# Identity turns by TensorE in the pauses at stage borders, semaphores of several stages cleared together, and the first mix squares ahead of attention's last store

## The reference, cut to what matters

```python
h = rmsnorm(x, g_mix[l])
proj = h @ w_in[l] + b_in[l]                       # queries, keys, values of both groups
...                                                # rotary on group A
oa = window_sink_gqa(qa, ka, va, sinks[l])
ob = chunk_relbias_attention(qb, kb, vb, rel_bias[l])
mix = jnp.concatenate([rmsnorm(oa, g_grp_a[l]), rmsnorm(ob, g_grp_b[l])], axis=-1)
x = x + mix @ w_out[l]
h = rmsnorm(x, g_cross[l])
x = x + memory_cross_attention(h, rmsnorm(mem, g_mem[l]), w_cq[l], w_ckv[l], w_co[l])
h = rmsnorm(x, g_ffn[l])
x = x + (jax.nn.silu(h @ w_gate[l]) * (h @ w_up[l])) @ w_down[l]
return rmsnorm(x, g_final)
```

## Time and profile before

| what | value |
|---|---|
| median of three runs | 2836.86 us (2836.58 to 2837.24) |
| the profiled execution's own time | 2837.78 us |
| its span, first to last instruction | 2836.0 us |
| PE busy | 2760.0 us, 97% of the span |
| DVE, ACT, POOL busy | 1587.8, 1064.3, 1065.7 us |
| mean granted TensorE clock | 0.990 |

### The profile page before, as it was taken

One profiled execution on the slowest core, in us unless ns is written; L12 is line 12 of the kernel. 1 busy time (PEld: TensorE's weight loads), 2 busy tenths in 40 slices (PEclk: granted clock), 3 DMA queues, 4 the chain that ended last, 5 costly groups with the idle time before them and its releaser, 6 DMA issues.

```text
span 2836.0 us, 39240 instructions
## 1 busy us (share of the span) xinstructions
PE 2760.0 (97%) x14112; PEld 2338.4 (82%) x14112; DVE 1587.8 (56%) x2721; ACT 1064.3 (38%) x2101; POOL 1065.7 (38%) x754
## 2 busy tenths in 40 slices
PE   8999999999999999999998999999999999999998
PEld 8888888899999787788887788888888887888876
DVE  3356664566688332333335766668866666654364
ACT  5433333366666221332334333334333332222342
POOL 7644454210000111321214645555654553552251
PEclk9999999999999999999999999999999999999999
DMA  7657768755664434122226333335432335644453
GB/s 269 239 166 261 258 210 260 209 145 149 165 141 112 176 133 155 75 67 80 79 82 210 109 93 104 112 112 186 126 98 92 106 112 191 234 140 145 142 177 126
DMA packets 244599, 428.47 MB, mean 151 GB/s; under 512 B 17856, under 2 KB 151488, under 8 KB 239168
## 3 DMA queue, kind: packets, MB, share of 16 engines
q1 hardware_dynamic: 207008, 358.43, 39.8%
q10 hardware_dynamic: 37408, 67.65, 7.6%
HBM read 285.50 MB, written 135.27 MB: 148 GB/s over the span
## 4 chain that ended last, share of the span: by engine, by line
PE 54%; DVE 2%; DMA 1%; POOL 1%; ACT 1%; issue 1%; SPq 0%; POOLq 0%; ACTq 0%; DVEq 0%
PE gu_acc L51 9%; PE gu_acc L52 9%; PE gu_acc L53 9%; PE down_acc L51 4%; PE down_acc L52 4%; PE down_acc L53 4%; PE cross_sum_s L51 2%; PE cross_sum_s L53 2%; PE cross_sum_s L52 2%; PE cross_sum_o L51 2%; PE cross_sum_o L53 2%; PE cross_sum_o L52 2%; DVE shared_m L2828 1%; DVE gu_t L2469 0%; PE cross_turned L2147 0%
## 5 line engine op out<-in xcount | busy, mean ns | idle before, releaser
L51 PE MATMUL gu_acc<-gu_t,shared_m 128*128 128x512 f32 x704 | 275.5, 391 | 4.8 <-DVE gu_t L2469 4.8
L53 PE MATMUL gu_acc<-gu_t,shared_m 128*128 128x512 f32 x704 | 274.9, 390 | 0.0
L52 PE MATMUL gu_acc<-gu_t,shared_m 128*128 128x512 f32 x704 | 274.9, 390 | 0.0
L338 POOL TENSOR_TENSOR front_wq_lo<-front_wq_raw,front_wq_hi 128x1024 fp32r<-128x1024 f32 x72 | 179.9, 2500 | 206.8 <-ACT front_wq_hi L334 206.6
L2412 ACT ACTIVATE shared_m<-kept_x 128x512 fp32r<-128x512 f32 x175 | 109.3, 628 | 211.6 <-PE gu_acc L53 191.0
L51 PEld LDWEIGHTS gu_acc<-gu_t,shared_m 128*128 128x128 f32 x704 | 132.8, 189 | 34.7 <-issue 4.4
L53 PEld LDWEIGHTS gu_acc<-gu_t,shared_m 128*128 128x128 f32 x704 | 132.7, 189 | 27.7
L52 PEld LDWEIGHTS gu_acc<-gu_t,shared_m 128*128 128x128 f32 x704 | 132.8, 189 | 27.3
L334 ACT ACTIVATE front_wq_hi<-front_wq_raw 128x1024 fp32r<-128x1024 f32 x72 | 76.2, 1058 | 191.9 <-PE qkv_acc L53 104.6
L51 PE MATMUL gu_acc<-shared_m 128*128 128x512 f32 x352 | 137.8, 391 | 2.9 <-POOL shared_m L2385 2.5
L52 PE MATMUL gu_acc<-shared_m 128*128 128x512 f32 x352 | 137.7, 391 | 0.0
(11 more groups left out here) (342 smaller groups left out, 7838.6 us busy)
## 6 DMA issues: line engine op xcount, KB each, us to landing
front_wq_raw<-in_w_in ACTq DMA_DIRECT2D x69, 512.0 KB, 4.2
ahead_w_even<-in_w_gate SPq DMA_DIRECT2D x44, 512.0 KB, 4.5
kept_x<-in_w_up SPq DMA_DIRECT2D x44, 512.0 KB, 4.3
a_d<-gu_a_mix SPq DMA_DIRECT2D x88, 256.0 KB, 3.2
a_d<-gu_a SPq DMA_DIRECT2D x66, 256.0 KB, 4.3
kept_x<-in_w_down SPq DMA_DIRECT2D x56, 256.0 KB, 4.7
shared_m<-a_d SPq DMA_DIRECT2D x19, 704.0 KB, 4.3
beside_turned<-a_d SPq DMA_DIRECT2D x19, 704.0 KB, 4.1
```

The costliest lines, as they stand in the source:

```text
L51: pe.matmul(out, l_hi, r_hi, start=first, stop=False)
L52: pe.matmul(out, l_hi, r_lo, start=False, stop=False)
L53: return pe.matmul(out, l_lo, r_hi, start=False, stop=last)
L338: pool.tensor_tensor(self.lo[:, i % Q_SLOTS, :], self.raw[:, i % Q_SLOTS, :], raw(self.hi[:, i % Q_SLOTS, :]), ALU.subtract).then_inc(self ...
```

## The change

`idle_turns` is new: it transposes the identity by itself into a PSUM bank that holds nothing needed. It is called in eight places, 182 turns in ten groups. A new class `Ends` gathers the semaphores of several rooms and clears them with one close; three of them stand where fourteen closes stood: after qkv, after mix, and at the program's end. Nothing is closed after products and after attention. And in attention's ACT stream `store_last(1)` moves behind the first squares of mix.

```diff
+class Ends:
+    def __init__(self, nc):
+        self.nc, self.sems = nc, []
+
+    def close(self):
+        self.nc.clear_and_free_semaphores(self.sems)
+        self.nc.all_engine_barrier()
...
     def sem(self, name):
         semaphore = self.nc.alloc_semaphore(f"{self.stage}_{name}")
-        self.sems.append(semaphore)
+        self.ends.sems.append(semaphore)
         return semaphore
-
-    def close(self):
-
-        self.nc.clear_and_free_semaphores(self.sems)
-        self.nc.all_engine_barrier()
...
+def idle_turns(pe, bank, ident, n):
+    for _ in range(n):
+        pe.transpose(bank[:, 0:P], ident[:, :], ident[:, :])
...
                 pe.wait_ge(s_ident, 2)
+                idle_turns(pe, acc[ACCS - 1], ident, 40)
                 for n in range(MT):
                     rows.turn(pe, ident[:, :], n)
+                    idle_turns(pe, acc[ACCS - 1], ident, 12 if n == 0 else 8)
                 pe.wait_ge(rows.s_lo, 2 * MT)
...
                         if a == TURN[t]:
                             rows.turn(pe, ident[:, :], MT + t)
+                pe.wait_ge(rows.s_lo, 2 * (MT + BT))
+                idle_turns(pe, rows.turned[0], ident, 18)
...
                         last.then_inc(s_vt, 1)
+                acc_free(TOTAL - ACCS)
+                idle_turns(pe, acc[TOTAL % ACCS], ident, 16)
...
-                store_last(1)
                 act.wait_ge(s_wlo, KT)
                 norm.start_act(act)
                 norm.act_square(act, 0, 0, 0)
+                store_last(1)
...
                     if step == NB:
                         norm.start_pe(pe)
+                after(pe, s_max, NB - 1)
+                idle_turns(pe, sum_s[NB % 2], ident, 30)
...
                 norm.pe_turn(pe, ident[:, :], 0, 0)
+                idle_turns(pe, acc[0], ident, 10)
...
                 over_pairs(pe, PAIRS, pair)
+                idle_turns(pe, norm.turned[0], ident, 10)
...
             def scores(n):
+                if n < 2:
+                    idle_turns(pe, sum_o[0], ident, 28 if n else 10)
                 pe.wait_ge(s_xlo, 2 * n + 2)
...
+    first_ends, middle_ends, last_ends = Ends(nc), Ends(nc), Ends(nc)
     with ExitStack() as later:
+        later.callback(last_ends.close)
...
+            first_ends.close()
...
+        middle_ends.close()
```

More of the change, by code:

```diff
@@ L58, in raw, with __init__ @@
     return ap.bitcast(F32)
+class Ends:
[4 more added lines that the diff above has]
+        self.nc.all_engine_barrier()
 class Room:
-    def __init__(self, nc, ctx, stage, side="left", ends=None):
-        self.nc, self.ctx, self.stage, self.sems, self.side = nc, ctx, stage, [], side
-        (ends or ctx).callback(self.close)
+    def __init__(self, nc, ctx, stage, ends, side="left"):
+        self.nc, self.ctx, self.stage, self.ends, self.side = nc, ctx, stage, ends, side
         self.s_gate = self.sem("s_gate")
@@ L342, in stage_products @@
 def stage_products(nc, mem, g_mem, g_cross_t, w_k, w_v, w_cq_t, w_co, m_d, n_d, x, g_mix, ident, gain_x, s_gain_x,
-                   h0, weights):
+                   h0, weights, ends):
     with ExitStack() as ctx:
-        room = Room(nc, ctx, "prod")
+        room = Room(nc, ctx, "prod", ends)
         rows = Rows(room)
@@ L1084, in __init__, with stage_attention @@
         self.norm = Norm(kept, 2, self.rows, self.s_rows, self.raw)
-def stage_attention(nc, qk_d, v_d, mix_d, bias_d, sinks8, weight, first, s_qk_stored, s_v_stored):
+def stage_attention(nc, qk_d, v_d, mix_d, bias_d, sinks8, weight, first, s_qk_stored, s_v_stored, ends):
     JOBS = [("b", h) for h in range(8)] + [("a", pp) for pp in range(N_PAIR)]
@@ L1158, in stage_attention @@
     with ExitStack() as ctx:
-        room = Room(nc, ctx, "att")
+        room = Room(nc, ctx, "att", ends)
         ident, norm = weight.ident, weight.norm
@@ L1509, in rows_of, with stage_mix @@
     return tensor[n * P:(n + 1) * P, :] if isinstance(n, int) else tensor[bass.ds(n * P, P), :]
-def stage_mix(nc, mix_d, x, weight, x2_d, m_sb, s_mlo, m_d, x2, s_x2, s_st, ident_next, s_ident_next):
+def stage_mix(nc, mix_d, x, weight, x2_d, m_sb, s_mlo, m_d, x2, s_x2, s_st, ident_next, s_ident_next, ends):
     with ExitStack() as ctx:
-        room = Room(nc, ctx, "mix")
+        room = Room(nc, ctx, "mix", ends)
         norm, ident = weight.norm, weight.ident
@@ L1757, in stage_cross @@
     with ExitStack() as ctx:
-        room = Room(nc, ctx, "cross", ends=ends)
+        room = Room(nc, ctx, "cross", ends)
         n_sb = [room.sb(f"n{part}", [P, KT, D], F32R) for part in range(2)]
@@ L2591, in stage_down @@
     with ExitStack() as ctx:
-        room = Room(nc, ctx, "down", ends=ends)
+        room = Room(nc, ctx, "down", ends)
         AHEAD = first.AHEAD
@@ L2931, in build @@
                 stage_products(nc, a["mem"], a["g_mem"], a["g_cross_t"], a["w_xk"], a["w_xv"], a["w_cq_t"], a["w_co"],
-                               m_d, n_d, a["x"], a["g_mix"], ident, gain, s_gain, h0, weights)
+                               m_d, n_d, a["x"], a["g_mix"], ident, gain, s_gain, h0, weights, first_ends)
                 stage_qkv(nc, a["x"], ident, gain, first, h0, weights, a["b_in"], a["positions"], a["freq"],
-                          a["rel_rev"], ext_d, bias_d, qk_d, v_d, s_qk_stored, s_v_stored)
-            weight = OutWeights(Room(nc, ctx, "wout", "right"), a["w_out"], a["g_grp"])
-            stage_attention(nc, qk_d, v_d, mix_d, bias_d, a["sinks"], weight, first, s_qk_stored, s_v_stored)
+                          a["rel_rev"], ext_d, bias_d, qk_d, v_d, s_qk_stored, s_v_stored, first_ends)
+            first_ends.close()
+            weight = OutWeights(Room(nc, ctx, "wout", middle_ends, "right"), a["w_out"], a["g_grp"])
+            stage_attention(nc, qk_d, v_d, mix_d, bias_d, a["sinks"], weight, first, s_qk_stored, s_v_stored,
+                            middle_ends)
             until_mix.close()
-            shared = Room(nc, later, "shared")
+            shared = Room(nc, later, "shared", last_ends)
             m_sb = [shared.sb(f"m{part}", [P, KT, D], F32R) for part in range(2)]
             s_mlo = shared.sem("s_m_lo")
-            kept = Room(nc, later, "kept")
+            kept = Room(nc, later, "kept", last_ends)
             x2 = kept.sb("x2", [P, XB, D])
@@ L2946, in build @@
             s_ident = kept.sem("s_ident")
-            stage_mix(nc, mix_d, a["x"], weight, x2_d, m_sb, s_mlo, m_d, x2, s_x2, s_x2_stored, ident, s_ident)
-        beside = Room(nc, later, "beside")
+            stage_mix(nc, mix_d, a["x"], weight, x2_d, m_sb, s_mlo, m_d, x2, s_x2, s_x2_stored, ident, s_ident,
+                      middle_ends)
+        middle_ends.close()
+        beside = Room(nc, later, "beside", last_ends)
         turned = [beside.sb(f"turned{part}", [P, 2, KT * P], F32R) for part in range(2)]
-        operands = GateUpOperands(shared, m_sb, Room(nc, later, "ahead", "right"), x2, turned, a["w_gate"], a["w_up"],
+        operands = GateUpOperands(shared, m_sb, Room(nc, later, "ahead", last_ends, "right"), x2, turned, a["w_gate"], a["w_up"],
                                   t_d)
         with nc.Block() as block:
-            cross = stage_cross(nc, block, later, ident, s_ident, turned, s_x2_stored, x2_d, x2, s_x2, m_sb, s_mlo, n_d,
+            cross = stage_cross(nc, block, last_ends, ident, s_ident, turned, s_x2_stored, x2_d, x2, s_x2, m_sb, s_mlo, n_d,
                                 a["g_ffn"], x3_d, t_d, operands)
             rows = DownOperands(shared, operands, a_d, a["w_down"])
-            gate_up = stage_gate_up(nc, block, later, cross, t_d, a["w_gate"], a["w_up"], a_d, operands, rows)
-            stage_down(nc, block, later, gate_up, a_d, x3_d, a["w_down"], a["g_final"], out, rows)
+            gate_up = stage_gate_up(nc, block, last_ends, cross, t_d, a["w_gate"], a["w_up"], a_d, operands, rows)
+            stage_down(nc, block, last_ends, gate_up, a_d, x3_d, a["w_down"], a["g_final"], out, rows)
 def by_tile(w, width):
```

10 lines of the change are left out of this document (5 added, 5 removed).

## The result

| | before | after |
|---|---|---|
| median of five runs each, us | 2836.86 | 2819.82 |
| lowest to highest, us | 2833.68 to 2838.34 | 2817.46 to 2824.29 |
| profiled execution, us | 2837.78 | 2817.46 |
| its span, us | 2836.0 | 2815.7 |
| PE busy in the span, us | 2760.0 | 2767.0 |

The ratio is 0.9943, with a 95% interval of 0.9932 to 0.9953: faster by 0.57%. The time forecast, 2818.2, is 1.6 us from the median. The profiled execution of after is the fastest of its five, so its gain of 20.3 us is above the median's 17.0. PE's busy time rose although the kernel is faster: 182 turns of the identity now count as busy.

What follows compares the result with a forecast made beforehand. PE was taken to bound the kernel: its work, its pauses and its half-clock stretches. Terms 3.35 + 2.65 + 1.75 + 4.0 + 3.2 + 3.75 = 18.7 us took the median from 2836.86 to 2818.2, range 2813.5 to 2824.5.

Steps and rivals of the forecast that it cites:

- The start: First products: full clock gives 2.7 us, faster real turns 0.7 (bounds 0 and 1.76); 3.35 in all, bounds 1.5 and 4.5.
- rival 3: All idle turns: turning an identity does not count as work for the clock; 2839.0 us, slower than before; chance 0.03.
- Products to qkv: Border products to qkv: the close going gives 0.6 us, the clock holding over a 2.1 us pause 2.05; sum 2.65.
- Rival 1: The clock falls in pauses left behind products, behind qkv and in mix: 2.05, 1.3, about 1.5 lost; 2823.0 us; chance 0.17.
- qkv to attention: Border qkv to attention: second close gone, 0.45 us; clock 1.3, between 0 and 3.1; sum 1.75.
- with a faster PE it is next: Attention's start: ACT, busy 4.67 of the 6.2 us low stretch, binds next, so 1.5 us lies above it; 1.3 taken.
- Attention to mix: Border attention to mix: start 2.7 us earlier, plus 1.3 of 3.35 from the clock because loads delay tile 2; 4.0.
- Rival 2: Mix: transfers don't bind, because loads start and land earlier with the whole border; 2.0 us more, 2816.2; chance 0.07.
- Mix to cross-attention and `scores(1)`: One close fewer 0.45 us, ten turns holding the clock 1.5, 28 turns before `scores(1)` 1.3; sum 3.2.
- The end: Program's end: seven closes become one, six at 0.63 us each are 3.75, bounds 3.2 and 3.9.
- rival 4: Closes: cost goes by semaphores cleared, so gathering saves only barriers, about half of 5.25 us; 2820.8; chance 0.05.
- Behind 1200 us: After 1160 us: shifted low stretches come or go, 2.5 us either way, 2815.7 or 2820.7; as a rival, chance 0.10.

Runs made afterwards that it cites:

- again: The changed kernel once more, unaltered, for a second profile and five more times: 2822.55 us, ratio 0.9944.
- nostart: The changed kernel without the 60 identity turns of the first stage: 2824.54 us, ratio 0.9957.
- noborder12: The changed kernel without the turns behind products (18) and behind qkv (16): 2827.6 us, ratio 0.9968.
- fill: The changed kernel with 24 instead of 16 turns behind qkv and 78 more in late pauses of PE: 2825.06 us, ratio 0.9957.
- fill_again: The same kernel as fill, run once more: 2819.81 us, one run.
- bars: The changed kernel with six more all-engine barriers at its end, which clear nothing: 2823.11 us, ratio 0.9950.
- best2: mixorder with 24 turns behind products and behind qkv, 20 ahead of mix, 14 ahead of down's second group: 2817.79 us, ratio 0.9932.
- mixorder: The changed kernel with ACT's squares and POOL's root of the next pair's first tile ahead of their `m_d` split parts: 2820.05 us, ratio 0.9940.
- nosmall: The changed kernel without the three groups of ten turns in mix, behind mix and in cross-attention: 2821.96 us, ratio 0.9955.

## Why the prediction was right, and what in it was not

**The sum** (18.7 forecast; 20.3 in the profiled pair, 17.0 in the medians). The six terms that the prediction filled came to 18.68. That this is so near is luck in part: the start and mix gave 0.5 and 0.4 more, cross-attention and the end 0.4 and 0.55 less. The ten runs of after and again have a median of 2821.2, 3.0 above the forecast. And the prediction called itself wrong if a low stretch stood behind any of the four borders; one does in after, behind qkv, and two in again. So the causes of the gains are those forecast, and the clock behind the pauses that are left is not as steady as forecast.

**The start** (3.35 forecast, 3.83). The clock part was right: ACT read the first block at 17.14 and the second 2.8 later. The split chain was undersized: I took 0.7 with a cap of 1.76, but the first product starts at 13.90 instead of 15.08 in before, 1.18 earlier. The 40 turns held up nothing: the first real turn waits 1.03 us for DVE behind them. They also settle rival 3. PE does nothing but turn the identity from 1.52 on, and the 40 take 6.23 us; at 0.21 from one to the next, the rate of half clock, they would take 8.5. The starts lie 0.21 apart up to the sixteenth turn and 0.11 from the seventeenth on, so turning an identity does bring the clock up. That the column of the clock is no guide at the start is seen in nostart too: 1.00 in the column and 31 matmuls in 5.5 us.

**Products to qkv** (2.65, 2.61). Right in this profile, with 0.6 for the close and 2.0 for the clock, but only where the clock holds. The table has 2.57 to 2.69 in six kernels with these turns and close, and 0.96 to 1.07 in four, where it fell. Rival 1 is real at this place. The split into 0.6 and 2.0 is not shown: noborder12, without the turns, has 1.05, which leaves 1.6 for them, because its low stretch ends sooner behind the first product than that of before did.

**qkv to attention** (1.75, 1.79). The agreement is luck: two misses cancel. The clock did fall, so rival 1 held in the profiled execution already. And a full clock is worth more than the 1.3 that I took from ACT's busy share: where it held (fill, fill_again, bars, and nostart with its 3.28 less the 0.83 lost inside qkv) the border gives 2.43 to 2.47, 1.9 to 2.0 beyond the close. The step that failed is "with a faster PE it is next".

**Attention to mix** (4.0, 4.44). PE's pause shrank from 6.76 to a first mix turn 3.88 us behind attention's last product, 2.9 gained against 2.7. That the turns and not DVE were late is shown by best2, by 0.3 us only: there DVE's scaling ends last, at 915.38, 0.7 ahead of mix's first turn. The wait at tile 2 came as forecast, 1.57 against 2.0, and mixorder shows its cause. Mix's first product starts at 918.75, forecast near 918.9. Rival 2, that the transfers don't bind, is refuted: in the nine kernels with the old order in mix and the new border the wait was 1.4 to 2.9.

**Mix to cross-attention and `scores(1)`** (3.2, 2.81). The ten turns are worth 1.56 (nosmall), as forecast; the close with `scores(1)` gave 1.25 instead of 1.75. The step that failed is the 0.45 for the close, which gave 0.15: without the ten turns PE's pause is 2.63 against 2.78 before. By source line on SP and POOL, before and then after:

```profile
L1532 SPq EVENT_SEMAPHORE  x1: 17/17/17, 1126.8 to 1126.8; - x1
...
L90 SPq EVENT_SEMAPHORE  x2: 17/17/17, 1127.4 to 1127.9; - x2
```

```profile
L1552 SPq EVENT_SEMAPHORE  x1: 17/17/17, 1114.5 to 1114.5; - x1
...
L69 SPq EVENT_SEMAPHORE  x1: 17/17/17, 1115.5 to 1115.5; - x1
...
L68 POOLq EVENT_SEMAPHORE_RANGE_CLEAR  x2: 68/188/308, 1114.7 to 1115.2; - x2
```

From the block's barrier to the end of the closes it takes 0.9 us in after and 1.1 before. The one close saves a barrier, but it clears what two borders had left: its two range clears take 0.38 us, the three of before took 0.22. `scores(1)` gave 1.2 of its 1.3: ACT's gain grows by 2.3 behind the wait and falls by 1.15 again before 1175 (in the time of before), in after and nosmall alike. That the value weights take it back, as the prediction supposed, isn't shown.

**The end** (3.75, 3.20). The bound of 3.2 was the value. I counted a close as one thing of 0.63; it is a barrier of 0.33 and clearing that grows with what is cleared. So rival 4 is right in part, here and at the border to cross-attention.

**Behind 1200 us** I put 0 with 2.5 either way. The kernels show -2.2 to +3.0 against the one trace of before, and after had 2.1. Without this and without the 0.44 lost in attention the profiled pair would stand at 20.3 - 2.1 + 0.44 = 18.6.

**Rival 1 was priced about right and given too small a chance.** Its 2.05 behind products measured 1.6 to 1.7; its 1.3 behind qkv 0.7 (after, against 2.45 where the clock held) to 2.3 (again); its 1.5 in mix some 1.4 (nostart's 1.78 against noborder12's 3.16, with like waits at tile 2). Of the eleven profiles with turns behind products and qkv, the clock was low behind products in four and behind qkv in seven. My forecast is the upper end of what the kernel gives, and the median of the second five runs, 2822.55, lies close to rival 1's 2823.0. The Trainium skill, TensorE: Matmul & The Clock Gate, section "What's actually happening", has the monitor's watch free-running; after and again, one program with two clocks behind one pause, agree. Of the 5.2 us between the spans of after and again, 1.65 and 1.67 lie at these two borders, 0.9 in mix, 1.0 behind 1500 us. But the clock is not all of the spread: the runs of after at 2817.46 and 2824.29 both have a mean granted clock of 0.997. A step of 0.001 is 5.6 us at half clock, or 2.6 us of time at 46%, so at least 4 of the 6.8 us between them come from something else, which no trace shows.

## What to carry to other kernels

Split a gain by stage, from matching instructions in two traces, before believing a median: single terms can be read to 0.1 us there, while the times of one kernel spread over 7 us. But take a second trace of the same kernel before you call a term a property of it: after and again, one program, differ by 1.7 us at two borders each. Filler work on PE is worth its place only where PE sets the pace behind the pause; where DVE's splits set it, a low clock is free. Look for what stands behind a late load in an engine's written order: moving two short instructions ahead of it took a 1.6 us wait away, which no faster border could.

## What the runs showed of the hardware that I had not expected

A pause of 2.1 us ahead of the same product brought the clock down in one execution and not in another. Turns of an identity by themselves, 40 from 1.52 us on, brought the clock up after sixteen of them in after. An all-engine barrier alone costs 0.33 us; a range clear costs 44 to 716 ns, and gathered it takes less than in parts: the ten at the end of before sum to 1.02 us, the one of after takes 0.72; over the whole program 18 take 1.99 us and the four of after 1.51. The two loads of 2 MB had landed 14.4 to 15.9 us after the first was issued in all kernels, whatever else had changed ahead of them.
